# A decoder layer on one core: v projected between the turned rows, q between the chunks, and four smaller moves

## The chip, the cores and the metric

The kernel runs on one core of one Trainium2 chip. The time is the device time of one execution, in microseconds (us). A core has TensorE for matrix products (PE in the profile, its weight loads PEld), VectorE (DVE), ScalarE (ACT), GpSimd (POOL), and SyncE (SP), which issues most of the transfers. All data are float32.

## The reference, cut to what matters

One layer over x of 1024 tokens by 1024 columns (T = D = 1024), and a memory of 256 tokens:

```
n = rmsnorm(x, g_mix);  x_ssm, u, v, q = split(n @ w_in)       # 512 columns each
y_a = glu(gelu(s5_ssm(x_ssm)) @ w_glu + b_glu)                 # diagonal state-space scan
y_b = gelu(u) * spatial(rmsnorm(gelu(v), g_sgu))               # mixing within chunks of 128 tokens
y_c = attention(q, rmsnorm(mem, g_mem) @ w_kv)                 # 4 heads of 128
h   = x + (sum_i sigmoid(n @ w_gate + b_gate)_i * (y_i @ w_branch_i)) @ w_out
xf  = rmsnorm(h, g_ffn)
groups, experts = xf @ w_group + b_group, xf @ w_router + b_router    # top group of 8, top 2 of its 8 experts
out = rmsnorm(h + weighted sum of 2 experts(xf), g_final)             # 64 experts, 1024 -> 512 -> 1024
```

## The kernel before, in words

The program is one block with a hand-written instruction order for each engine; semaphores join them. Tokens go in NT = 8 tiles of 128. PSUM has four banks that ScalarE empties (`act_bank`) and four that VectorE empties (`dve_bank`). Every bank filling is a numbered job: `act_jobs` and `dve_jobs` list them in order (`plan`), job n uses bank n mod 4, and TensorE waits before job n until job n - 3 is drained. So the order of the list is the order on TensorE, on the draining engine, and in the waits.

**Head.** SP loads the eight tiles of x, small parameters and `w_ssm`. ScalarE takes squares and a root of four tiles at a time, VectorE normalizes them, TensorE turns each tile into two banks, and ScalarE and VectorE copy one bank each into `nT`. After all eight, TensorE turns the raw lambda (job "lam"); VectorE then computes the discretized parameters, with one visit to ScalarE for the sine; GpSimd raises the phases and fills `Lmat`. TensorE meanwhile projects x_ssm (job "ssm_proj", 8 blocks), then makes the convolution kernel (job "kernel", line 793), then tile 0 of v, then "bin" (it waits for `states_in_made` of GpSimd, line 630). SP copies the kernel into `toep`, after which the four chunks run: `chunk_in` (turn, then the state product of line 824) and `chunk_out` (line 833 with `toep`, line 842 with the state). VectorE runs `rotate`, `add_out` and `make_state` for each chunk in turn. Tiles 1 to 4 of v stand between chunks 1 and 0's output, tile 5 after the last chunk, tiles 6 and 7 after the turning of y ("ysT"), and all eight blocks of q after those. Then come the GLU, the memory's norm and turning, k and vm.

**Attention.** TensorE makes k (4 blocks) and both blocks of vm, waits until they are drained, and then makes the scores of tile 0; the softmax of tile 0 (VectorE, ScalarE, VectorE) follows, and only then the transposes of its probabilities. Later tiles have the scores of the next tile and a block of u between them.

**Gates, branches, output.** After a loop of eight gate steps, TensorE waits for `merged`, both halves of w_out and the router's weights, and then projects: `project(i)` is tile i of merged @ w_out (32 matrix instructions). For each tile: `project(i + 1)`, `rank(i - 1)` (the count of earlier tokens of the same expert, by a triangular matrix), the turning of the normed tile, its logits. VectorE: norm of tile i, `residual(i + 1)`, `place(i - 1)` (the token's row in the expert table), then `choose(i)` once the logits are there. The running sum `chosen` of the chosen experts enters the rank.

**Experts.** A unit is up to 32 tokens of one expert. Weights stream into four slots; SP refills a slot when TensorE has read it (`gu_ready`, `y_ready`).

The order that the change touches stands in this table of jobs:

```
(act_jobs, (("x", NT), ("ssm_proj", STEP), ("v0", 1), ("bin", 8), ("in0", 2), ("in1", 2), ("v1", 4),
            ("in2", 2), ("in3", 2), ("v5", 1), ("ysT", STEP // 2), ("v6", 2), ("q", 2 * KW),
            ("glu_b", 6), ("mem", NM), ("glu_b6", 2), ("k", HEADS), ("vm", NM),
            ("scores", 2 * NT + 2 * KW), ("gates", 6 * KD), ("xfT", 2 * NT))),
```

Of the kernel before, what the change touches and what calls it, by code (L numbers as in the profile page):

```python
# [27 lines left out]
ALU = mybir.AluOpType  # L28
# [75 lines left out]
def program(nc, x, mem, g_mix, g_mem, w_in, w_gate, b_gate, lam_re, lam_im, log_dt, b_re, b_im,  # L104
# [3 lines left out]
    with ctx:  # L108
# [52 lines left out]
        x_rows = mid_store[:, :].rearrange("p (i d) -> p i d", i=NT)  # L161
# [39 lines left out]
        w_ssm, w_glu_s = tiles(7, KD), tiles(4, KW)  # L201
# [42 lines left out]
        block_at, row_at = now[:, 342:344], now[:, 344:346]  # L244
# [80 lines left out]
        for family, rows in (  # L325
            (act_jobs, (("x", NT), ("ssm_proj", STEP), ("v0", 1), ("bin", 8), ("in0", 2), ("in1", 2), ("v1", 4),
                        ("in2", 2), ("in3", 2), ("v5", 1), ("ysT", STEP // 2), ("v6", 2), ("q", 2 * KW),
                        ("glu_b", 6), ("mem", NM), ("glu_b6", 2), ("k", HEADS), ("vm", NM),
                        ("scores", 2 * NT + 2 * KW), ("gates", 6 * KD), ("xfT", 2 * NT))),
# [13 lines left out]

        def v_job(i):
            return job(act_jobs, "v0") if i == 0 else job(act_jobs, f"v{1 if i < 5 else 5 if i < 6 else 6}",
                                                          i - (1 if i < 5 else 5 if i < 6 else 6))
# [4 lines left out]
        def score_job(i):  # L351

            return job(act_jobs, "scores", 3 * i - 1 if i else 0)

        def u_job(i):
            return job(act_jobs, "scores", 3 * i + 4 if i < NT - 1 else 3 * i + 2)
# [15 lines left out]
        def logits_job(i):  # L372

            return job(dve_jobs, "out", 4 * i + 4 if i < NT - 1 else 4 * i + 2)

        def rank_job(i):

            return job(dve_jobs, "out", 4 * i + 7 if i < NT - 2 else 29 + 2 * (i - NT + 2))
# [23 lines left out]
        def _(sp):  # L402
            x_tiles = x[0].rearrange("(i p) d -> i p d", p=P)
            for i in range(NT):
                sp.dma_start(x_rows[:, i], x_tiles[i]).then_inc(x_row_loaded[i], 16)

            def columns(w, a, n):
                return w[:, a:a + n].rearrange("(k p) n -> p k n", p=P)

# [7 lines left out]
            sp.dma_start(w_ssm, columns(w_in[0], 0, W)).then_inc(w_loaded["ssm"], 16)  # L417
# [4 lines left out]
            for n, v in enumerate((c_re, c_im)):  # L422
                for z in range(2):
                    for g2 in range(2):
                        sp.dma_start(c_raw[:, 2 * n + z, 64 * g2:64 * g2 + 64],
                                      v[0].rearrange("(g z j) h p -> z g (j h) p", z=2, g=2)[z, g2]
                                      ).then_inc(ssm_loaded, 16)
            sp.dma_start(lane_row[:, :], bc(d_skip[0], 0, P)).then_inc(bias_loaded, 16)
# [9 lines left out]
            sp.wait_ge(act_filled, jobs_end(act_jobs, "ssm_proj"))  # L438
            sp.dma_start(w_v, columns(w_in[0], 2 * W, W)).then_inc(w_loaded["v"], 16)
# [17 lines left out]
            sp.wait_ge(act_filled, jobs_end(act_jobs, "q"))  # L457
# [18 lines left out]
            sp.wait_ge(act_filled, jobs_end(act_jobs, "vm"))  # L476
# [102 lines left out]
        def _(pool):  # L579
# [71 lines left out]
            pool.wait_ge(act_filled, jobs_end(act_jobs, "vm"))  # L651
# [85 lines left out]
        def _(pe):  # L737
# [25 lines left out]
            for i in range(NT):  # L763
                pe.wait_ge(row_normed[i % 2], i // 2 + 1)
                bank = act_bank_for(job(act_jobs, "x", i))
                turn(bank, [x_rows[:, i, k * P:(k + 1) * P] for k in range(4)]).then_inc(act_filled, 1)
                bank = dve_bank_for(job(dve_jobs, "x", i))
                turn(bank, [x_rows[:, i, k * P:(k + 1) * P] for k in range(4, 8)]).then_inc(dve_filled, 1)

            pe.wait_ge(act_drained, NT)  # L770
            pe.wait_ge(dve_drained, NT)
# [4 lines left out]
            for s in range(STEP):  # L776
                if s == 2:
                    pe.wait_ge(ssm_loaded, 16 * N_SSM)
                    bank = dve_bank_for(job(dve_jobs, "c"))
                    turn(bank, [c_raw[:, n] for n in range(4)]).then_inc(dve_filled, 1)  # L780
                bank = act_bank_for(job(act_jobs, "ssm_proj", s))
                ins = accumulate(bank[:, :], [(nT_phase[:, k, s], w_ssm[:, k]) for k in range(KD)])
                ins.then_inc(act_filled, 1)
# [3 lines left out]
            for q in range(QUADS):  # L787
                for g2 in range(2):
# [6 lines left out]
                    ins.then_inc(dve_filled, 1)  # L795

            pe.wait_ge(w_loaded["v"], 16)

            def v_tiles(a, b):
                for i in range(a, b):  # L800
                    bank = act_bank_for(v_job(i))
                    ins = accumulate(bank[:, :], [(nT[:, k, i * P:(i + 1) * P], w_v[:, k]) for k in range(KD)])
                    ins.then_inc(act_filled, 1)

            v_tiles(0, 1)
# [40 lines left out]

            chunk_in(0)
            chunk_in(1)
            v_tiles(1, 5)
# [4 lines left out]
            chunk_in(3)  # L854
            chunk_out(2)
            chunk_out(3)
            v_tiles(5, 6)
# [7 lines left out]
            v_tiles(6, NT)  # L865

# [901 lines left out]
```

## Time and profile before

| | |
|---|---|
| median of 3 runs | 2270.11 us (2269.36 to 2274.81) |
| profiled execution, its own time | 2267.0 us |
| its span | 2265.1 us |
| granted TensorE clock, mean | 0.908 of full speed |
| busy: TensorE matrix, VectorE, ScalarE, GpSimd | 1794.9, 475.1, 254.8, 258.2 us |
| head and mixers, up to the last gate step | 0 to 965.5 us |
| output projection and routing | 965.5 to about 1146 us |
| experts | about 1146 to 2199 us |
| last norm and store | 2199 to 2265 us |

Times in the rows are counted from the start of the span. A duration in a row is that of the whole group of instructions ("x32" is 32 of them); a float32 product of one pair of operands stands as two matrix instructions. The bracket at the end of a row is the engine's idle time before it and what ended it. TensorE runs at one of two levels, 1.2 and 2.4 GHz, which the column PEclk shows as 0.50 and 1.00.

### The profile page before, as it was taken

The numbers are of one execution on the slowest core, as the hardware profiler recorded it, in microseconds if no ns is written. First come the engines' busy times: TensorE is split into PE (matmuls) and PEld (weight loads), VectorE is DVE, ScalarE is ACT, GpSimd is POOL, SyncE is SP. The second block draws the span as 40 slices with busy tenths as digits, with TensorE's granted clock in tenths as the row PEclk, the third lists the DMA queues.
The fourth block names the chain that finished last, engine by engine and source line by source line (L and its number), as shares of the span: only waits on it lengthen the run. The fifth ranks groups of instructions, "written<-read, shape, count | busy, mean of one in ns | idle before, by whom it ended". The sixth has DMA issues, their size and how long they took to land.

```text
span 2265.1 us, 38820 instructions
## 1 busy us (share of the span) xinstructions
PE 1794.9 (79%) x13852; PEld 1000.1 (44%) x13853; DVE 475.1 (21%) x1140; ACT 254.8 (11%) x538; POOL 258.2 (11%) x377
## 2 busy tenths in 40 slices
PE   6998999999999999989757777777777776455550
PEld 4655445654444444435434444444444453232220
DVE  6554012431011111025521001010011010000006
ACT  3112212410000000001100000000000000000003
POOL 2940000000000000001111111111111110000014
PEclk9998999999999999999879889899999899676775
DMA  6412013011111110055479999989999979999985
GB/s 224 122 40 107 4 36 105 23 44 42 42 42 42 42 42 29 8 189 197 184 275 400 409 409 406 401 308 374 405 397 369 391 283 419 415 416 420 422 334 210
DMA packets 152743, 510.96 MB, mean 226 GB/s; under 512 B 34352, under 2 KB 84016, under 8 KB 135792
## 3 DMA queue, kind: packets, MB, share of 16 engines
q1 hardware_dynamic: 122096, 461.36, 52.5%
q0 software_dynamic: 8768, 27.02, 3.4%
q10 hardware_dynamic: 21840, 22.06, 2.8%
q8 instruction: 23, 0.38, 0.1%
q14 instruction: 16, 0.13, 0.0%
HBM read 479.71 MB, written 34.35 MB: 227 GB/s over the span
## 4 chain that ended last, share of the span: by engine, by line
PE 56%; DMA 18%; SPq 11%; issue 5%; DVE 5%; ACTq 2%; ACT 1%; POOL 1%; POOLq 0%; DVEq 0%
PE act_bank L751 27%; PE dve_bank L751 14%; DMA gain_b<-xf_rows,gather_idx 11%; SPq L553 5%; PE act_bank L1045 4%; DMA unit_results<-spatialT 3%; SPq L499 3%; PE dve_bank L758 3%; PE act_bank L1059 2%; SPq L503 2%; DMA tokens<-expert_token_table 2%; PE dve_bank L1059 2%; ACTq L1247 1%; DMA unit_results<-lane_row 1%; DVE unit L1311 1%
## 5 line engine op out<-in xcount | busy, mean ns | idle before, releaser
L751 PE MATMUL act_bank<-norm_store,unit 128*128 128x512 f32 x1024 | 448.9, 592 | 0.0
L751 PEld LDWEIGHTS act_bank<-norm_store,unit 128*128 128x128 f32 x1024 | 194.6, 190 | 241.1 <-issue 240.6
L1045 PE MATMUL act_bank<-unit,gain_a 128*32 128x256 f32 x3520 | 207.3, 388 | 26.2 <-issue 26.1
L758 PE MATMUL dve_bank<-ident,gain_b 32*128 32x32 f32 x808 | 73.8, 235 | 179.8 <-DMA gain_b<-xf_rows,gather_idx 179.6
L1059 PE MATMUL act_bank<-unit,gain_a 128*32 128x256 f32 x2208 | 175.4, 471 | 39.6 <-DVE gain_a L1717 39.6
L1715 DVE TENSOR_TENSOR gain_a<-gain_a,act_bank 128x128 f32<-128x128 f32 x100 | 28.8, 288 | 757.0 <-ACT gain_a L1240 739.0
L1045 PEld LDWEIGHTS act_bank<-unit,gain_a 128*32 128x32 f32 x3520 | 123.6, 113 | 111.4 <-issue 53.5
L758 PEld LDWEIGHTS dve_bank<-ident,gain_b 32*128 32x128 f32 x808 | 64.1, 151 | 223.8 <-issue 223.8
L1059 PEld LDWEIGHTS act_bank<-unit,gain_a 128*32 128x32 f32 x2208 | 90.2, 130 | 97.4 <-issue 81.4
L1593 DVE TENSOR_TENSOR rows_store<-dve_bank,rows_store 128x512 f32<-128x512 f32 x48 | 33.2, 692 | 431.1 <-PE dve_bank L751 431.1
L751 PE MATMUL dve_bank<-unit,mid_store 128*128 128x512 f32 x256 | 113.4, 602 | 9.0 <-DMA unit<-in_w_router 9.0
L751 PE MATMUL dve_bank<-unit,unit 128*128 128x512 f32 x256 | 115.1, 592 | 0.0
L688 POOL COPY gather_idx<-tokens 32x1 int32 x100 | 17.8, 178 | 841.7 <-PE dve_bank L758 580.8
L751 PE MATMUL act_bank<-unit,norm_store 128*128 128x512 f32 x256 | 113.5, 603 | 0.0
L751 PE MATMUL dve_bank<-unit 128*128 128x512 f32 (+1 forms) x320 | 104.0, 474 | 6.2 <-ACT unit L1092 6.2
L692 POOL DMA_INDIRECT gain_b<-xf_rows,gather_idx x101 | 94.7, 938 | 83.4 <-POOL gather_idx L688 83.4
L1045 PE MATMUL act_bank<-norm_store,gain_a 128*32 128x256 f32 x1344 | 83.3, 403 | 21.6 <-issue 21.6
L1045 PE MATMUL act_bank<-mid_store,gain_a 128*32 128x256 f32 x1536 | 91.5, 391 | 10.1 <-issue 10.1
L1059 PE MATMUL dve_bank<-rows_store,gain_a 128*32 128x256 f32 x992 | 75.2, 454 | 17.8 <-DVE gain_a L1717 17.8
L751 PEld LDWEIGHTS act_bank<-unit,norm_store 128*128 128x128 f32 x256 | 64.7, 255 | 44.9 <-issue 30.5
L1205 ACT ACTIVATE rows_store<-act_bank,gate_bias_now 128x512 f32<-128x512 f32 x48 | 33.0, 687 | 417.6 <-PE act_bank L751 417.5
L751 PEld LDWEIGHTS dve_bank<-unit,mid_store 128*128 128x128 f32 x256 | 48.9, 193 | 68.9 <-issue 68.9
(227 smaller groups left out, 1474.5 us busy)
## 6 DMA issues: line engine op xcount, KB each, us to landing
unit<-in_w SPq DMA_DIRECT2D x112, 2048.0 KB
norm_store<-in_w SPq DMA_DIRECT2D x32, 2048.0 KB
mid_store<-in_w SPq DMA_DIRECT2D x32, 2048.0 KB
rows_store<-in_w SPq DMA_DIRECT2D x16, 2048.0 KB
unit<-in_w_gate SPq DMA_DIRECT2D x24, 512.0 KB, 5.2
unit<-in_w_in SPq DMA_DIRECT2D x4, 2048.0 KB, 8.9
unit_results<-unit POOLq DMA_DIRECT2D x4, 2048.0 KB, 13.4
unit_results<-spatialT ACTq DMA_DIRECT2D x220, 32.0 KB
```

The costliest lines, as they stand in the source:

```text
L499: sp.dma_start(w13[s][:, z].rearrange("p k n -> p (k n)"), w_up[z].rearrange("e (p k) n -> p (e k n)", p=P)).then_inc(up_loaded[s], 16)
L503: sp.dma_start(w2s[s], w_down.rearrange("e (k p) n -> p (e k) n", p=P)).then_inc(down_loaded[s], 16)
L553: sp.dma_start(tokens[:, s], table_of[bass.ds(e, 1)].rearrange("e p n -> (e p) n")).then_inc(tokens_loaded[s], 16)
L692: pool.indirect_dma_start(xg, None, xf_dram, bass.IndirectOffsetOnAxis(ap=gather_idx[:, 0:1], axis=0), bounds_check=T - 1, oob_is_err=Fals ...
L751: ins = nc.tensor.matmul(out_, stationary, moving, start=first and n == 0, stop=n == len(pairs) - 1)
L758: ins = nc.tensor.transpose(bank[:, n * rows:(n + 1) * rows], block_, ident[0:rows, 0:rows])
L1045: ins = nc.tensor.matmul(act_bank[0][h * CAP:(h + 1) * CAP, 0:2 * FQ].rearrange("t (w n) -> t w n", w=2), xT[:, k], w13[s][:, :, k, h * FQ ...
L1059: ins = nc.tensor.matmul(y_bank[s][z * CAP:(z + 1) * CAP, 0:DQ], hidT[:, j], w2s[s][:, j, z * DQ:(z + 1) * DQ], start=j == 0, stop=j == QU ...
L1205: drained(nc.scalar.activation(gates[n % 4], act_bank[g % 4][:, :], ACT.Sigmoid, bias=gate_bias_now[:, s, i:i + 1]))
L1247: act.dma_start(y_dram[bass.ds(u * CAP, CAP), z * DQ:(z + 1) * DQ], y_rows[s][z * CAP:(z + 1) * CAP]).then_inc(per_slot["y_stored"][s], 16)
L1593: v.tensor_tensor(parts[i], dve_bank[b % 4][:, :], gates[n % 4], ALU.mult).then_inc(dve_drained, 1)
L1715: v.tensor_tensor(hid, silu_g, act_bank[0][:, FQ:2 * FQ], ALU.mult).then_inc(per_slot["hid_ready"][s], 1)
```

## The change

1. `w_v` is loaded after the fourth tile of x; `w_ssm` goes to another buffer (unit 5) and is loaded last of the early parameters. Tile i of x lies at another place of `mid_store`, so that v's rows don't overwrite rows that are still to be turned.
2. TensorE: turn x 0, 1; v 0; turn x 2, 3; v 1; turn x 4 to 7; lam; v 2 to 4; the turning of C; v 5 to 7; ssm_proj 0 to 2; kernel; ssm_proj 3 to 7; bin. ScalarE and VectorE follow this order: ScalarE takes the squares of tiles 4 to 7 after it has copied x 0 and 1, and the sine after v 2; VectorE copies x 0 and x 1 between norms, and x 2 to 7 after the last norm.
3. q: blocks 0 and 1 stand where v 1 to 4 stood; block 2 ahead of the output of chunk 2, block 3 ahead of that of chunk 3, block 4 after it, blocks 5 to 7 after ysT. The memory's squares follow block 5.
4. vm block 1 comes after the scores of tile 0; the wait for it stands ahead of its first use.
5. The wait for the router's weights moves from ahead of the projections to ahead of the first logits. `rank(i - 1)` moves behind the turning of tile i.
6. The norm of tile 7 comes ahead of the choice of tile 6; tile 6's rank and place come after the choice of tile 7, and tile 7's rank adds tile 6's choice by further products with `ones` in place of `chosen`. `row_at` gets two buffers.

The core of the diff:

```diff
-            (act_jobs, (("x", NT), ("ssm_proj", STEP), ("v0", 1), ("bin", 8), ("in0", 2), ("in1", 2), ("v1", 4),
-                        ("in2", 2), ("in3", 2), ("v5", 1), ("ysT", STEP // 2), ("v6", 2), ("q", 2 * KW),
+            (act_jobs, (("x0", 2), ("v0", 1), ("x2", 2), ("v1", 1), ("x4", 4), ("v2", 6), ("ssm_proj", STEP),
+                        ("bin", 8), ("in0", 2), ("in1", 2), ("q0", 2), ("in2", 2), ("in3", 2), ("q2", 1), ("q3", 1),
+                        ("q4", 1), ("ysT", STEP // 2), ("q5", 3),
...
             for i in range(NT):
-                sp.dma_start(x_rows[:, i], x_tiles[i]).then_inc(x_row_loaded[i], 16)
+                if i == 4:
+                    sp.dma_start(w_v, columns(w_in[0], 2 * W, W)).then_inc(w_loaded["v"], 16)
+                sp.dma_start(x_rows[i], x_tiles[i]).then_inc(x_row_loaded[i], 16)
...
+            x_turn(0, 2)
+            pe.wait_ge(w_loaded["v"], 16)
+            v_tiles(0, 1)
+            x_turn(2, 4)
+            v_tiles(1, 2)
+            x_turn(4, NT)
             pe.wait_ge(lam_loaded, 16 * 4)
             bank = dve_bank_for(job(dve_jobs, "lam"))
             turn(bank, [lam_raw[:, n] for n in range(2)], PAIRS).then_inc(dve_filled, 1)
+            v_tiles(2, 5)
...
             chunk_in(0)
             chunk_in(1)
-            v_tiles(1, 5)
+            pe.wait_ge(w_loaded["q"], 16)
+            q_part(0, 2)
             pe.wait_ge(toep_made, 16 * STEP)
             chunk_out(0)
             chunk_in(2)
             chunk_out(1)
             chunk_in(3)
+            q_part(2, 3)
             chunk_out(2)
+            q_part(3, 4)
             chunk_out(3)
-            v_tiles(5, 6)
+            q_part(4, 5)
...
+            vm_part(0)
+            pe.wait_ge(act_drained, jobs_end(act_jobs, "k"))
             scores(0)
+            vm_part(1)
...
             pe.wait_ge(w_loaded["out_hi"], 16)
-            pe.wait_ge(w_loaded["route"], 32)
...
+                if i == NT - 1:
+                    for c in range(2):
+                        nc.tensor.matmul(bank[:, 0:E], ones, hot[:, i - 1, c], start=False, stop=False)
...
-                if i:
-                    rank(i - 1)
                 pe.wait_ge(xf_made, i + 1)
...
+                if i and i < NT - 1:
+                    rank(i - 1)
+                if i == 0:
+                    pe.wait_ge(w_loaded["route"], 32)
...
             for i in range(NT):
+                if i < NT - 1:
+                    row_norm(i)
                     residual(i + 1)
+                    if i:
+                        place(i - 1)
+                if i == NT - 2:
+                    row_norm(NT - 1)
```

## Rows read from the trace of the kernel before

**Rows 1.** Stretches: length; busy PE, PEld, DVE, ACT, POOL; PEclk, DMA share, GB/s.
```profile
32.39:106.41 74.02, 74.02 (x278) 52.94 (x276) 50.91 (x127) 7.79 (x12) 56.09 (x81) 1.00 0.42 149
151.96:199.64 47.68, 35.11 (x273) 32.54 (x272) 35.56 (x54) 6.93 (x12) 6.34 (x5) 0.79 0.08 28
365.16:377.74 12.58, 7.28 (x26) 6.04 (x26) 5.03 (x8) 3.81 (x10) 0.78 (x1) 0.73 0.55 147
400.00:960.00 560.00, 560.00 (x1472) 263.72 (x1471) 94.89 (x143) 63.50 (x107) 1.51 (x8) 1.00 0.13 36
965.50:1004.04 38.54, 29.58 (x65) 12.99 (x65) 7.20 (x14) 2.73 (x4) 1.54 (x4) 0.87 0.64 239
1111.74:1139.36 27.62, 13.71 (x73) 12.31 (x71) 17.30 (x73) 5.16 (x9) 3.88 (x4) 0.62 0.97 383
1163.00:2199.00 1036.00, 721.75 (x10448) 428.80 (x10440) 91.10 (x300) 66.18 (x200) 110.39 (x198) 0.88 0.98 389
```

**Rows 2.** Timeline of PE in the head: start, duration, group, idle before.
```profile
16.58 1.09 PE L758 MATMUL act_bank<-ident,mid_store 128*128 128x128 f32 x4 [16.58 <-DVE mid_store L1287]
...
116.23 3.68 PE L824 MATMUL dve_bank<-unit,unit 128*64 128x128 f32 x32 [3.63 <-ACT unit L1092]
...
122.50 1.97 PE L824 MATMUL dve_bank<-unit,unit 128*64 128x128 f32 x32 [0.69 <-ACT unit L1092]
...
151.96 1.95 PE L833 MATMUL dve_bank<-unit,unit 128*128 128x128 f32 x16
...
193.21 6.50 PE L842 MATMUL dve_bank<-unit,gain_b 64*128 64x128 f32 x32 [8.12 <-DVE gain_b L1481]
```

**Rows 3.** Timelines of DVE and POOL in the head, columns as in rows 2.
```profile
32.50 0.19 DVE L1335 COPY unit<-dve_bank 128x32 f32<-128x32 f32 x1 [0.40 <-PE dve_bank L758]
...
81.97 0.06 DVE L1435 MEMSET table_mark<- 128x1 f32 x1
...
129.90 0.20 DVE L1451 MEMSET gain_b<- 128x4 f32 x2 [29.77 <-POOLq L633]
...
157.38 0.69 DVE L1488 TENSOR_TENSOR mid_store<-mid_store,dve_bank 128x512 f32<-128x512 f32 x1 [0.66 <-PE dve_bank L842]
...
192.46 0.69 DVE L1481 TENSOR_TENSOR gain_b<-unit 128x508 f32<-128x508 f32 x1
...
107.19 0.72 POOL L600 TENSOR_TENSOR unit<-gain_b 128x256 f32<-128x256 f32 x1
```

**Rows 4.** The chain that ended last, head: start, duration, what.
```profile
88.28 11.15 PE dve_bank L793 x128
```

**Rows 5.** Timeline of SP's queue, then transfers to 420 us: KB each, us to landing.
```profile
113.02 0.63 SPq L447 DMA_DIRECT2D unit<-in_w_in  x1
...
unit<-in_w_in SPq DMA_DIRECT2D x4, 2048.0 KB, 8.9
```

**Rows 6.** Timeline of PE at the first scores.
```profile
372.46 1.94 PE L758 MATMUL dve_bank<-ident,rows_store 128*128 128x128 f32 x8 [4.61 <-issue]
```

**Rows 7.** Timelines of SP and PE where the projections begin.
```profile
967.95 0.82 SPq L511 DMA_DIRECT2D rows_store<-in_x  x2
...
974.50 29.70 PE L751 MATMUL dve_bank<-unit,mid_store 128*128 128x512 f32 x64 [8.96 <-DMA unit<-in_w_router]
```

**Rows 8.** Timeline of PE, one turn of the routing loop.
```profile
1021.44 0.55 PE L1000 MATMUL dve_bank<-unit 128*128 128x64 f32 x4
...
1022.05 1.04 PE L758 MATMUL act_bank<-ident,rows_store 128*128 128x128 f32 x8
1023.84 2.00 PE L751 MATMUL dve_bank<-unit 128*128 128x72 f32 x16 [0.74 <-ACT unit L1092]
```

**Rows 9.** Timeline of PE and the chain at the last tile.
```profile
1126.93 3.69 PE L751 MATMUL dve_bank<-unit 128*128 128x72 f32 x16 [0.75 <-ACT unit L1092]
...
1134.69 1.11 PE L1000 MATMUL dve_bank<-unit 128*128 128x64 f32 x4 [4.07 <-DVE unit L1649]
...
1139.19 0.18 DVE table_row L1631
```

More of the change, by code:

```diff
@@ L243, in program @@
         top, mark = now[:, 338:340], now[:, 340:342]
-        block_at, row_at = now[:, 342:344], now[:, 344:346]
+        block_at, row_base = now[:, 342:344], [now[:, 344 + 2 * n:346 + 2 * n] for n in range(2)]
         spatial_raw = mid_store[:, 0:512].rearrange("t (h s) -> t h s", h=HEADS)
@@ L774, in _ @@
             turn(bank, [lam_raw[:, n] for n in range(2)], PAIRS).then_inc(dve_filled, 1)
-            pe.wait_ge(w_loaded["ssm"], 16)
[L776 to L783, printed above, removed]
+            v_tiles(2, 5)
+            pe.wait_ge(ssm_loaded, 16 * N_SSM)
+            bank = dve_bank_for(job(dve_jobs, "c"))
+            turn(bank, [c_raw[:, n] for n in range(4)]).then_inc(dve_filled, 1)
+            v_tiles(5, NT)
+            pe.wait_ge(w_loaded["ssm"], 16)
+            ssm_proj(0, 3)
             pe.wait_ge(tables_made, 1)
@@ L795, in _ @@
                     ins.then_inc(dve_filled, 1)
[L797 to L805, printed above, removed]
+            ssm_proj(3, STEP)
             pe.wait_ge(states_in_made, 1)
@@ L845, in chunk_out, with q_part @@
                     ins.then_inc(dve_filled, 1)
+            def q_part(a, b):
+                for n in range(a, b):
+                    h, z = n // 2, n % 2
+                    bank = act_bank_for(q_job(n))
+                    ins = accumulate(bank[:, :], [(w_q[:, k, h * P:(h + 1) * P], nT[:, k, z * HALF:(z + 1) * HALF])
+                                                  for k in range(KD)])
+                    ins.then_inc(act_filled, 1)
             chunk_in(0)
             chunk_in(1)
-            v_tiles(1, 5)
+            pe.wait_ge(w_loaded["q"], 16)
+            q_part(0, 2)
             pe.wait_ge(toep_made, 16 * STEP)
@@ L1022, in _ @@
                 ins.then_inc(dve_filled, 1)
+            rank(NT - 2)
             rank(NT - 1)
@@ L1171, in _ @@
                 drain("k", h, kT[:, h], width=MEM)
-            for i in range(NM):
-                drain("vm", i, vm[:, i])
+            drain("vm0", 0, vm[:, 0])
             def exponents(i):
@@ L1654, in choose, with row_norm @@
                 tt(exp_in[:, 64 + i:65 + i], top[:, 1:2], top[:, 0:1], ALU.subtract)
[L1655 removed]
+                ts(row_base[i % 2], mark, -float(T), ALU.mult, float(T * FIRST), ALU.add)
             step(v.memset(chosen, 0.0))
             dve.wait_ge(masks_made, 4)
[L1659 to L1660 removed]
+            def row_norm(i):
                 s = i % 2
@@ L1665, in _ @@
                      s, gain_a[:, :].rearrange("p (q k) -> p k q", k=KD)).then_inc(xf_made, 1)
-                if i + 1 < NT:
+            residual(0)
+            for i in range(NT):
+                if i < NT - 1:
+                    row_norm(i)
                     residual(i + 1)
-                if i:
-                    place(i - 1)
+                    if i:
+                        place(i - 1)
+                if i == NT - 2:
+                    row_norm(NT - 1)
                 n = logits_job(i)
```

195 lines of the change are left out of this document (113 added, 82 removed).

## The prediction

> **What bounds the kernel now.** I read the slices of the page first (three regimes), then busy time by stretch [rows 1], then the timelines of each engine at the places where TensorE is not busy. Up to 965.5 us the bound is TensorE: in 400 to 960 us it is busy 560.00 of 560.00 us at full clock, and nothing that the change does can shorten that. What can go are holes and half-clock time around them. In the stretch of the first projections (74.02 us) there is no hole, but ahead of it TensorE starts at 16.58 with transposes at half rate (1.09 us for four) and reaches the first projection only at 32.39 [rows 1, 2]. The chunks (151.96 to 199.64) have 12.6 us of holes at a mean clock of 0.79; the first scores 5.3 us of 12.58 at 0.73; the routing 9.0 us ahead of its first projection; the last tile 13.9 us of 27.62 at 0.62 [rows 1]. From 1163 to 2199 the DMA share is 0.98 [rows 1]: the weight stream sets the experts' pace. It restarts from TensorE's reading of the slots, so an earlier start moves it as a whole.
>
> **1 and 2, v between the turned rows.** The products stay the same; their order fills the holes. One block of v, ssm_proj or q costs 6.9 us: the stretch of 74.02 us holds nine of them, the turning of C (0.4) and the kernel, 11.15 [rows 1, 4]. Turning one tile of x costs 0.9 (eight transposes 1.04, overlapped) once the clock is up [rows 8]. New clock: turn x 0, 1 at 16.6 to 19.7 (as before), v 0 to 26.6, x 2, 3 to 28.3, v 1 to 35.2, x 4 to 7 to 38.7, lam 39.0. `w_v` stands fifth, behind the same 2 MB plus its own 2, so it lands when the eighth tile of x did, which I estimate at 16 us; that is before v 0. The squares of tiles 4 to 7 come later on ScalarE (about 19.8 to 25), and the norms end near 31, ahead of the 35.2 at which x 4 is wanted. What is late next is lam: VectorE copies it at 39.6 where it did at 32.50 [rows 3]. So VectorE's parameters and GpSimd's chain come 7.1 us later: `tables_made` 89 instead of 82, `states_in_made` 115 instead of 107.9, phases 137 instead of 129.9 [rows 3]. The extra visit to ScalarE for the sine (after v 2, drained at 46.5) lies under VectorE's own work.
>
> TensorE then runs without a wait: v 2 to 4 to 59.7, C 60.1, v 5 to 7 to 80.8, ssm_proj 0 to 2 to 101.5, kernel (wants 89) to 112.6, ssm_proj 3 to 7 to 147.1, bin (wants 115) 3.5 to 150.6. `toep` is filled by then: SP's copies began 1 us after the kernel and were done 15 us later. The wait of 3.63 us for it at 116.23, and the half clock behind it (3.68 for what took 1.97 at 122.50) go away [rows 2].
>
> **3, q in the holes.** Both `chunk_in` end near 158.5. SP issues `w_q` only when bin is filled (its buffer holds `Lmat`): 150.6 + 0.6 + 8.9 = 160.1 [rows 5], a new wait of 1.6 us, with q 0, 1 and the output of chunk 0 queued behind it. q 0, 1 end at 173.9, and a chunk's output costs 1.95 + 3.25 (half of 6.50, which ran at half clock) = 5.2 [rows 2]: 179.1. VectorE's rotate, state, rotate took 129.90 to 152.1 = 22.2; from its first input at 154.1 that ends at 176.3. So TensorE sets Y = 179.1, where before the same point was 157.3 [rows 3]. From there: in2, out1, in3 take 18.0 as before (157.3 to 175.3, VectorE's pace and 5 us of half clock in it); then q 2 to Y + 24.9, out2 to 30.1, q 3 to 37.0, out3 to 42.2, q 4 to 49.1, ysT (3.5) to 52.6, q 5 to 7 to 73.3. VectorE's last state comes at Y + 35.9 (192.46 + 0.7 against 157.3) [rows 3], under q 3. The GLU begins at 252.4 where it did at 280.8: **28.4 us less**. Bounds: 22, if one more q block runs at half clock; 34, if `w_q` is in time, the half clock in the chunks goes and the start of v is as I have it.
>
> A rule stands against this term. The Trainium skill, "TensorE: Matmul & The Clock Gate", section "Part 1: The HAM clock gate", says that the throttled state is the default and that activity releases it; the trace agrees (half rate at 16.58, and again at 116.23 behind a hole of 3.63 us). By it the small, broken products of the chunks could hold the low level into q 2 and q 3, and the gain would be some 14 us smaller. That is rival A below, worked out from the rows.
>
> **4, vm after the first scores.** The stretch from vm's end to u holds 5.30 us of idle time, and eight transposes (1.94) and eight score products at half clock [rows 1, 6]. With vm 1 (6.9 us) between, the softmax (4.61 us after the scores) is covered. Idle 5.3 and half of the 1.94 and of the 3.62 us of scores, 2.8: **8.1 us less**. Without the cover (ScalarE's exponentials later than vm 1) 2 us would be left to pay: 6 to 8.5.
>
> **5, the router's weights.** The inputs of the projections are ready when SP is released, at 967.95; they begin at 974.50 behind the route weights [rows 7]: 6.5. The 64 products took 29.70; at 6.9 us for 16 they take 27.5, so 2.2 more if the clock has not fallen. It fell during the hole (0.87 over the stretch [rows 1]); 2.5 us of hole are left, between the 0.69 after which the rate stayed high and 3.63 after which it was half [rows 2]; I take half: **7.6 us less** (6.5 to 8.7). The residual's x lands far ahead of its use.
>
> `rank` costs 0.6 (1021.44 to 1022.05), and 0.74 us of idle time wait for ScalarE between turning and logits [rows 8]. Behind the turning, rank lies in that hole, six times: **3.7 us less**. `place` comes 1.5 us later on VectorE, which has 5 us of idle time a tile. Bounds: 0 and 4.4.
>
> **6, the last tile.** With t the end of the last projection (1111.74): before, place 7 ends at t + 27.6 (1139.19 + 0.18) [rows 9]. After: turning, rank 5, logits 6 end at t + 3.4; place 5 at t + 4.0, norm 7 (3.3) at t + 7.3, choice 6 (4.6) at t + 11.9; TensorE: turning 7 at half clock to t + 9.3, copy 0.7, logits 7 (3.7 at half clock [rows 9]) to t + 13.7; tile 7's second choice 4.0 later, t + 17.7; place 6 (1.9) behind it, under the rank; rank 7: 2.83 before, with eight more matrix instructions of 0.21 at half clock 4.5, t + 22.3; place 7 (1.8) t + 24.1. **3.5 us less**. Bounds: 1 (the scatter of tile 6 goes out only 4 us before that of tile 7, and transfers are at 0.97) and 6 (full clock).
>
> **Sum.** 28.4 + 8.1 + 7.6 + 3.7 + 3.5 = 51.3 us, against the profiled execution's 2267.0: 2215.7. The median of the runs is 3.1 above that execution, so I give 2218 for it (2270.1 less 51.3 is 2218.8). With all low bounds the gain is 35.5, with all high ones 61.6.
>
> **Rivals.** A: the low clock lasts. If q 2 and q 3 run at 1.2 GHz, each costs 6.9 more; gain 37.5, time 2232.5. For it: clock 0.79 over the chunks, and half rate after holes of only 0.7 us. Against it: 6.9 us of dense products lie in each, and the rate at 16.58 was up 3 us later. B: the gain ahead of the experts is given back, since the stream of weights runs at 0.98 of the DMA for 1036 us and would be paced from a point that does not move: time 2268 to 2270, no change. Against it: the refills wait for `gu_ready`, which moves. C, the other side: the dense head runs at half clock. From 19.7 to 147.1 TensorE has sixteen blocks; at 1.2 GHz each costs 6.9 more. It decides from 7.4 blocks on (51.3 / 6.9); all sixteen would cost 110, time 2329. Against it: 560 us at 1.00 with no hole [rows 1]. D: the change is worth more, since holes between transposes and copies that I have left stay below what they were: 2204 to 2209.
>
> **How the numbers follow.** Forecast 0.78 (2209 to 2226), A 0.12, D 0.06, B 0.02, C 0.02. A difference under 0.3% (7 us) is about what a measurement of this kernel can't tell from none. Forecast, A and D are all faster by more: 0.96; B 0.02; C 0.02. The range goes from D's upper end to A: 2207 to 2232.
>
> **What would show it.** Right: first v block at about 20; kernel at 101; no hole over 2 us between 20 and 160; GLU at 252; scores of tile 0 followed by a block into `act_bank` with no hole; projections 2 us after the last merge; first expert unit some 51 us earlier, and the length from there to the end unchanged within 2 us. Wrong: PEclk under 0.8 over the chunks with a q block of 13 us; VectorE waiting for phases past 154; `w_q` landing after 165; x 4 to 7 still unnormed at 35.

## The result and the profile after

The changed kernel takes 2219.14 us (median of 4 runs, 2215.21 to 2220.36); the kernel before takes 2269.74 (4 runs on the same chip, 2268.81 to 2274.81). The ratio is 0.9774, with a 95% interval of 0.9761 to 0.9786: 50.6 us less, where 51.3 were summed up and 2218 was forecast. The profiled execution took 2220.36 us, its span 2218.3 (before 2267.0 and 2265.1), so the two traces stand 46.8 us apart. Of all runs told below one, of tok_first, took 2556.55 us at a granted clock of 0.724, where its others had 0.91 to 0.92; its median and its ratio leave it out.

Timeline of PE in the head of the changed kernel; columns as in [rows 2].

```profile
16.55 1.09 PE L764 MATMUL act_bank<-ident,mid_store 128*128 128x128 f32 x4 [16.55 <-DVE mid_store L1331]
...
19.99 8.25 PE L757 MATMUL act_bank<-unit,norm_store 128*128 128x512 f32 x16
...
148.63 3.66 PE L764 MATMUL act_bank<-ident,unit 128*128 128x128 f32 x32
...
154.38 1.97 PE L839 MATMUL dve_bank<-unit,unit 128*64 128x128 f32 x32 [1.22 <-ACT unit L1119]
...
160.66 14.00 PE L757 MATMUL act_bank<-norm_store,unit 128*128 128x512 f32 x32 [0.58 <-DMA unit<-in_w_in]
...
176.37 3.50 PE L857 MATMUL dve_bank<-unit,gain_b 64*128 64x128 f32 x32
...
193.98 7.13 PE L757 MATMUL act_bank<-norm_store,unit 128*128 128x512 f32 x16
...
229.63 20.77 PE L757 MATMUL act_bank<-norm_store,unit 128*128 128x512 f32 x48
250.23 1.02 PE L757 MATMUL act_bank<-unit 128*128 128x512 f32 x2
```

The first block of v starts at 19.99, and there is no wait until the first state product (1.22 us, line 839). The hole of 3.63 us and the half clock behind it [rows 2] are gone. The first block takes 8.25 us and the next ones 7.0: the four transposes ahead of it took 1.06 us, as at 16.55, and those behind it 0.60, so its first products still ran at the slower rate. The wait for `w_q` is 0.58 us. The last row is the first product of the GLU: 250.23, where before it was at 280.8.

Timelines of DVE in the changed kernel, columns as in [rows 3]: lam, the parameters' last step, the end of the wait for the phases.

```profile
40.99 0.18 DVE L1391 COPY unit<-dve_bank 128x32 f32<-128x32 f32 x1
...
90.37 0.06 DVE L1491 MEMSET table_mark<- 128x1 f32 x1
...
138.28 0.19 DVE L1507 MEMSET gain_b<- 128x4 f32 x2 [23.43 <-POOLq L639]
```

Each comes 8.4 to 8.5 us later than its row in [rows 3]. TensorE makes the kernel from 102.94 on and bin from 148.63, so neither waits for them.

Stretches of the changed kernel, columns as in [rows 1]: head, chunks, first scores, first projections, last tile, first expert product to near the end of the experts.

```profile
20.00:160.00 140.00, 138.04 (x551) 88.66 (x550) 66.22 (x153) 27.95 (x48) 82.80 (x104) 1.00 0.37 107
150.60:222.00 71.40, 65.57 (x439) 46.02 (x438) 55.72 (x88) 16.52 (x34) 11.80 (x10) 1.00 0.16 55
329.00:339.50 10.50, 10.50 (x37) 6.04 (x36) 5.03 (x9) 3.22 (x10) 0.78 (x1) 1.00 0.17 50
926.60:958.40 31.80, 29.36 (x66) 12.86 (x66) 7.20 (x14) 2.73 (x4) 1.53 (x4) 0.95 0.79 290
1063.00:1087.31 24.31, 15.11 (x81) 14.05 (x79) 16.85 (x71) 5.16 (x9) 3.87 (x4) 0.65 0.97 387
1108.32:2152.00 1043.68, 740.75 (x10500) 436.58 (x10500) 90.90 (x300) 66.03 (x200) 110.30 (x199) 0.86 0.97 387
```

The chunks run at 1.00 with 5.8 us without a product, where 47.68 us had 12.6 us of holes at a clock of 0.79 [rows 1]. The first scores have no hole left. The last tile looks as before: 0.65 against 0.62, and full transfers.

Timelines of the changed kernel where the projections begin, at the last tile and behind it: PE, DVE, ACT's queue, SP's queue, POOL.

```profile
929.08 29.43 PE L757 MATMUL dve_bank<-unit,mid_store 128*128 128x512 f32 x64 [2.44 <-DVE mid_store L1653]
...
1063.00 1.04 PE L764 MATMUL act_bank<-ident,rows_store 128*128 128x128 f32 x8
...
1070.38 1.97 PE L764 MATMUL act_bank<-ident,rows_store 128*128 128x128 f32 x8 [3.54 <-DVE rows_store L1331]
1073.10 3.69 PE L757 MATMUL dve_bank<-unit 128*128 128x72 f32 x16 [0.75 <-ACT unit L1119]
...
1087.14 0.17 DVE L1688 CAST table_row<-spatialT 128x2 int32<-128x2 f32 x1
...
1088.85 0.97 POOL L685 DMA_INDIRECT expert_token_table<-token_id,table_row  x1 [0.30 <-issue]
1093.50 0.33 SPq L505 DMA_DIRECT2D unit<-in_w  x1
1093.99 1.85 ACTq L1273 DMA_DIRECT2D tokens<-expert_token_table  x4
1101.20 0.18 POOL L694 COPY gather_idx<-tokens 32x1 int32 x1 [11.38 <-DMA tokens<-expert_token_table]
...
1108.32 5.10 PE L1072 MATMUL act_bank<-norm_store,gain_a 128*32 128x256 f32 x64 [1.95 <-issue]
```

The table's last row comes at 1087.14, 52.05 us earlier than in [rows 9]. From there to the first expert product it takes 21.2 us, where the kernel before took 18.0 (1139.19 to 1157.19): 3.2 us are given back. The lists of tokens (line 1273, 16 KB in four transfers) are issued 0.49 us behind 2 MB of expert 3's weights (SP, line 505) and are in use only at 1101.20. In the kernel before the tokens went out at 1144.33, ahead of those weights at 1145.55, and were in use at 1146.41. From the first expert product to the end of the span it is 1110.0 us (before 1107.9).

By parts, each as the shrinkage of its stretch between the two traces: head 30.5; GLU to the first block of u 8.3 (96.83 to 88.56); u to the end of the first 64 projection products 6.9 (6.6 of waiting, 0.3 of products); six turns of the routing loop 3.7 (108.35 to 104.65); the turning of tile 6 to the table's last row 2.7 (26.98 to 24.32). Together 52.1, less 3.2 before the experts and 2.1 in them: 46.8.

### The profile page after: what moved, and what is told of

It is laid out like the page before. It is cut to its first block, busy times and chain, and to the rows that moved or that the text cites. A ratio compares the mean times of both kernels' runs of the same rounds, so it can differ in the third digit from the quotient of the medians.

```text
span 2218.3 us, 38841 instructions
## 1 busy us (share of the span) xinstructions
PE 1793.4 (81%) x13860; PEld 994.4 (45%) x13861; DVE 473.7 (21%) x1138; ACT 255.6 (12%) x539; POOL 256.9 (12%) x377
## 4 chain that ended last, share of the span: by engine, by line
PE 57%; DMA 18%; SPq 11%; issue 5%; DVE 4%; ACTq 3%; ACT 1%; POOL 1%; POOLq 0%; DVEq 0%
PE act_bank L757 27%; PE dve_bank L757 14%; DMA gain_b<-xf_rows,gather_idx 10%; SPq L559 5%; PE act_bank L1072 5%; DMA unit_results<-spatialT 3%; SPq L505 3%; PE act_bank L1086 3%; PE dve_bank L764 3%; DMA tokens<-expert_token_table 2%; PE dve_bank L1086 2%; SPq L509 2%; ACTq L1291 2%; DMA unit_results<-lane_row 1%; PE act_bank L764 1%
## 5 line engine op out<-in xcount | busy, mean ns | idle before, releaser
L1072 PE MATMUL act_bank<-unit,gain_a 128*32 128x256 f32 x3520 | 211.4, 393 | 22.1 <-issue 21.8
L1086 PE MATMUL act_bank<-unit,gain_a 128*32 128x256 f32 x2208 | 183.0, 487 | 39.7 <-DVE gain_a L1780 38.5
```

Source lines behind the costliest of these rows:

```text
L1072: ins = nc.tensor.matmul(act_bank[0][h * CAP:(h + 1) * CAP, 0:2 * FQ].rearrange("t (w n) -> t w n", w=2), xT[:, k], w13[s][:, :, k, h * FQ ...
L1086: ins = nc.tensor.matmul(y_bank[s][z * CAP:(z + 1) * CAP, 0:DQ], hidT[:, j], w2s[s][:, j, z * DQ:(z + 1) * DQ], start=j == 0, stop=j == QU ...
```

## The experiments

The length of the experts' stage differs by up to 11 us between these executions, and doesn't follow the edits. So I read each run at three marks of its trace, and take the time of the kernel as the last test. Ratios are to the kernel before, measured on the same chip beside each; the medians come from different chips and compare only through them. The diffs show the core of each edit; the lists of jobs and the order of the draining engines follow it.

| kernel | median us | ratio (95%) | GLU starts | GLU to last table row | row to first expert product | from there to the end |
|---|---|---|---|---|---|---|
| before | 2269.74 | 1 | 280.77 | 858.4 | 18.0 | 1107.9 |
| changed | 2219.14 | 0.9774 (0.9761 to 0.9786) | 250.23 | 836.9 | 21.2 | 1110.0 |
| head_only | 2242.22 | 0.9875 (0.9846 to 0.9905) | 253.33 | 857.3 | 18.1 | 1112.2 |
| no_vm | 2227.35 | 0.9821 (0.9797 to 0.9845) | 249.02 | 844.8 | 21.2 | 1106.8 |
| no_route | 2227.46 | 0.9818 (0.9793 to 0.9843) | 249.65 | 844.2 | 21.2 | 1111.8 |
| no_rank | 2220.70 | 0.9789 (0.9764 to 0.9813) | 249.39 | 839.2 | 21.4 | 1109.6 |
| no_last | 2212.75 | 0.9770 (0.9742 to 0.9798) | 249.63 | 838.0 | 18.0 | 1105.0 |
| q_late | 2236.43 | 0.9863 (0.9835 to 0.9890) | 267.29 | 835.2 | 21.0 | 1111.6 |
| v_late | 2225.68 | 0.9819 (0.9794 to 0.9844) | 256.46 | 835.2 | 21.1 | 1112.8 |
| tok_first | 2214.09 | 0.9766 (0.9734 to 0.9798) | 249.51 | 836.9 | 15.9 | 1111.9 |
| tok_first_all | 2218.23 | 0.9780 (0.9746 to 0.9814) | 251.86 | 836.9 | 13.2 | 1115.7 |
| warm_project | 2218.68 | 0.9777 (0.9744 to 0.9810) | 248.49 | 835.0 | 21.0 | 1113.0 |
| warm_last | 2217.09 | 0.9779 (0.9740 to 0.9818) | 249.54 | 833.4 | 21.2 | 1106.4 |
| best | 2216.81 | 0.9763 (0.9745 to 0.9781) | 252.71 | 831.3 | 19.8 | 1114.8 |

### The head alone, and each later part undone

**head_only** keeps parts 1 to 3 and undoes the rest.

> Parts 1 to 3 alone (v, q, their loads); parts 4, 5 and 6 are undone. If the terms add up as stages that follow each other (theory), the GLU begins at 250.2 as in the changed kernel, the gain is 30.5 us and the time 2239 us. If the experts' stream gives back what is won ahead of it (rival), the first expert unit comes 30 us earlier and the end does not: 2255 us or more.

The head is worth 27.4 us here, about half of all; it ends 3.1 us later than in the changed kernel, though its code is the same. Timeline of PE in head_only, in the chunks:

```profile
186.13 4.46 PE L857 MATMUL dve_bank<-unit,gain_b 64*128 64x128 f32 x32 [1.10 <-DVE gain_b L1533]
...
193.17 3.68 PE L839 MATMUL dve_bank<-unit,unit 128*64 128x128 f32 x32 [0.69 <-ACT unit L1115]
196.78 8.07 PE L757 MATMUL act_bank<-norm_store,unit 128*128 128x512 f32 x16
```

In the changed kernel these groups took 3.50, 1.97 and 7.13. The clock fell between the chunks' small products, behind holes of about 1 us, and was back within one block of q. Of the twelve kernels here that have the chunks in this order, nine profiled executions ran them at 1.00 and start the GLU at 248.5 to 250.2 (v_late at 256.5), and three at 0.93 (head_only, tok_first_all, best) and start it at 251.9 to 253.3. None of their edits touches the chunks. The head is worth 27 to 32 us by that (280.77 less 253.33 and less 248.49).

**no_vm** makes both vm blocks ahead of the scores again:

```diff
             vm_part(0)
-            pe.wait_ge(act_drained, jobs_end(act_jobs, "k"))
-            scores(0)
             vm_part(1)
+            pe.wait_ge(act_drained, jobs_end(act_jobs, "vm1"))
+            scores(0)
```

> The changed kernel with both vm blocks ahead of the first scores again. Theory: the wait for the softmax of tile 0 (4.6 us), the wait for vm's drain (0.7) and half clock behind it (2.8) come back: 8.3 us slower than the changed kernel, 2227.4 us. Rival (the softmax was mostly covered otherwise): under 3 us.

Timeline of PE in no_vm at the first scores:

```profile
340.70 1.94 PE L764 MATMUL dve_bank<-ident,rows_store 128*128 128x128 f32 x8 [4.61 <-issue]
342.44 3.26 PE L935 MATMUL act_bank<-mid_store,unit 128*128 128x256 f32 x8
```

The hole of 4.61 us is back, digit for digit as in [rows 6], and the last table row comes 7.9 us later: the term of 8.1 holds.

**no_route** waits for the router's weights ahead of the projections again.

```diff
             pe.wait_ge(w_loaded["out_hi"], 16)
+            pe.wait_ge(w_loaded["route"], 32)
...
-                if i == 0:
-                    pe.wait_ge(w_loaded["route"], 32)
```

> The changed kernel with the wait for the router's weights ahead of the projections again. Theory: projections begin 6.5 us later, and the clock loss is about the same in both (the 64 products took 29.43 us with the short hole, 29.70 with the long one): 6.8 us slower, 2225.9 us. Rival: since the residual and norm of tile 0 have slack, under 3 us.

The projections wait 8.88 us where the changed kernel waits 2.44, and their 64 products take 30.27 us where they took 29.43; the row comes 7.3 us later. The term of 7.6 holds.

**no_rank** puts `rank(i - 1)` back ahead of the turning, for the first six.

```diff
+                if i and i < NT - 1:
+                    rank(i - 1)
                 pe.wait_ge(xf_made, i + 1)
...
-                if i and i < NT - 1:
-                    rank(i - 1)
```

> The changed kernel with rank(i - 1) ahead of the turning for tiles 1 to 6 again. Theory: 0.6 us a tile, six tiles: 3.7 us slower, 2222.8 us, and the period of the routing loop 18.07 us instead of 17.46. Rival (VectorE's place sets the pace): none.

The six turns take 108.37 us instead of 104.65, 3.7 as expected. But 1.4 us are won back behind them: without rank 5 between turning 6 and its logits the tail takes 22.9 us, not 24.3. Place 5 and the norm of tile 7 come earlier, so the turning of tile 7 begins 6.5 us behind that of tile 6 and not 7.4, and it takes 1.41 us and not 1.97. The part is worth 2.3 us net, and by the ratios nothing that can be told from zero.

**no_last** undoes part 6: the norm of tile 7 after the choice of tile 6, one rank and one place ahead, no further products with `ones`.

```diff
-                if i < NT - 1:
-                    row_norm(i)
+                row_norm(i)
+                if i < NT - 1:
                     residual(i + 1)
-                    if i:
-                        place(i - 1)
-                if i == NT - 2:
-                    row_norm(NT - 1)
+                if i:
+                    place(i - 1)
```

> The changed kernel with part 6 undone (norm of tile 7 after the choice of tile 6, rank and place of tile 6 ahead of the logits of tile 7). In the changed trace the last place ends 2.7 us earlier counted from the last turning of tile 6, but the scatter takes 5.1 us instead of 3.4 and the first token lists 6.8 instead of 1.6. Theory: SP now issues 2 MB of weights (rows_picked) just ahead of ScalarE's token loads and they queue behind it, which gives the 2.7 back: the time without part 6 is the same as with it, within 2 us of 2219, with token lists landing in under 2.5 us. Rival (the slow landing is chance): 2.7 us slower, 2221.8 us, and token lists as slow.

The row comes 1.1 us later, but the first expert product is earlier by 2.0 us from the GLU's start (856.0 against 858.1). Timelines of no_last: ACT's queue, SP's queue, POOL.

```profile
1093.01 1.77 ACTq L1270 DMA_DIRECT2D tokens<-expert_token_table  x4
1094.00 0.33 SPq L505 DMA_DIRECT2D unit<-in_w  x1
1094.99 0.18 POOL L694 COPY gather_idx<-tokens 32x1 int32 x1 [4.66 <-DMA tokens<-expert_token_table]
```

The tokens leave 1 us ahead of the weights and are in use 2.0 us after they were issued, not 7.2. The other traces agree. In the eight kernels here that issue those weights first (the changed kernel, no_vm, no_route, no_rank, q_late, v_late, warm_project, warm_last) the lists are in use 6.3 to 7.3 us after their issue; in the kernel before, head_only and no_last, where they go first, 2.0 to 2.2. Part 6 as made gains nothing that these runs can tell: it turns a race for the transfer engines the wrong way round.

### The two halves of the head

**q_late** puts blocks 2 to 4 of q behind the last chunk's output; **v_late** turns all eight tiles of x before the first block of v (the first lines of the diff; q_late is the rest).

```diff
-            x_turn(0, 2)
-            pe.wait_ge(w_loaded["v"], 16)
-            v_tiles(0, 1)
-            x_turn(2, 4)
-            v_tiles(1, 2)
-            x_turn(4, NT)
+            x_turn(0, NT)
...
-            v_tiles(2, 5)
+            v_tiles(0, 5)
...
             chunk_in(3)
-            q_part(2, 3)
             chunk_out(2)
-            q_part(3, 4)
             chunk_out(3)
-            q_part(4, 5)
+            q_part(2, 5)
```

> The changed kernel with q 2, 3 and 4 all behind the last chunk, none in the holes. Theory: the holes of the chunks come back with the low clock: the last chunk's output ends 42 us after that of chunk 0 (39.5 with q in the holes) and two more blocks follow it: 16 us slower, 2235 us. Rival (the clock does not fall, since it depends on what ran ahead of the chunks): 10 to 12 us slower, PEclk at 1.00 over the chunks.

> The changed kernel with all eight tiles of x turned ahead of the first block of v; VectorE keeps its order. Theory: TensorE idles for VectorE's norms as before the change and reaches lam at 32 instead of 40, but has two blocks of v (13.8 us) still to do: 5.5 us slower, 2224.6 us. Rival (the earlier lam shortens a later wait): no change.

q_late starts the GLU 17.1 us later, v_late 6.2. Timeline of PE in q_late at the last chunk, then in v_late at the turning of tile 4:

```profile
213.98 6.51 PE L857 MATMUL dve_bank<-unit,gain_b 64*128 64x128 f32 x32 [8.12 <-DVE gain_b L1533]
```

```profile
27.41 1.12 PE L764 MATMUL act_bank<-ident,mid_store 128*128 128x128 f32 x4 [4.12 <-DVE mid_store L1325]
```

The hole of 8.12 us ahead of the last output and its 6.5 us at half clock are back just as in [rows 2]. Some 17 of the head's 30 us are the q blocks in the chunks' holes, 6 the v blocks between the turned rows. The other 7 or so were not undone singly: there the hole of 3.63 us and its half clock lie, and v 1 to 4 that left the chunks.

### The tokens ahead of the weights

**tok_first** makes SP wait for the first gather before it issues the last 2 MB of expert 3; **tok_first_all** does so with all its 6 MB.

```diff
             sp.wait_ge(rows_picked, 1)
+            sp.wait_ge(tok_gathered, 16)
             expert_up(up, 3, halves=(1,))
```

In tok_first_all the loads that stand ahead of `rows_picked` move too:

```diff
-            expert_up(up, 3, halves=(0,))
...
-            expert_down(down, 3)
             sp.wait_ge(rows_picked, 1)
+            sp.wait_ge(tok_gathered, 16)
-            expert_up(up, 3, halves=(1,))
+            expert_up(up, 3)
+            expert_down(down, 3)
```

> The changed kernel with the last 2 MB of expert 3's weights issued only after the tokens of the first unit are gathered. Theory (the token lists queue behind these 2 MB): the lists land in about 1.6 us instead of 6.8, the gather stays at about 3 us, the first expert unit comes 5 us earlier, 2214 us. Rival (the 2 MB then lie in the stretch where the stream is the bound): the first unit comes earlier but the end by less than 1 us.

> The changed kernel with all of expert 3's weights (both halves of the up matrices and the down matrix, 6 MB) issued only once the token gather has landed; in the changed kernel 4 of the 6 MB are issued ahead of the scatter and 2 MB just ahead of the token loads. Theory (the weights' transfers hold up the scatter and the token lists): the scatter lands in about 3 us, not 4.9 to 5.1, token lists in 1.6, gather in 3 or less, and the first expert product starts some 2 us earlier after the table's last row than with only the last 2 MB held back (15.9 us there, 21.0 in the changed kernel), so about 13.5 to 14. Rival 1: the 6 MB arrive too late for expert 3 and the stage from the first expert product to the end, 1104 to 1112 us so far, becomes longer than 1113; the total is then no better than that with 2 MB held back (2215) or worse than the changed kernel (2219). Rival 2: the scatter is slow for its own sake and stays at 4.9.

With the last 2 MB held back the first expert product starts 15.9 us after the last row, and 13.2 us with all 6 MB held back: the scatter, 1.2 us from the end of its issue to the tokens' issue where it was 4.2, was held up too. Timelines of tok_first, ACT's queue and POOL:

```profile
1093.07 1.77 ACTq L1274 DMA_DIRECT2D tokens<-expert_token_table  x4
...
1095.07 0.18 POOL L695 COPY gather_idx<-tokens 32x1 int32 x1 [5.99 <-DMA tokens<-expert_token_table]
```

Timelines of tok_first_all: POOL and ACT's queue.

```profile
1090.43 0.96 POOL L685 DMA_INDIRECT expert_token_table<-token_id,table_row  x1 [0.30 <-issue]
...
1092.59 1.77 ACTq L1273 DMA_DIRECT2D tokens<-expert_token_table  x4
...
1094.75 0.18 POOL L694 COPY gather_idx<-tokens 32x1 int32 x1 [3.36 <-DMA tokens<-expert_token_table]
```

But the kernel gains nothing that can be measured: 0.9780 and 0.9766 against 0.9774, intervals that overlap. In tok_first_all the way from there to the end, 1115.7 us, is the longest of all, as rival 1 had it: 4 MB sent later would be missing in a stage whose transfers are 0.97 busy. The stage's own spread leaves that a possible cause and not a shown one.

### TensorE kept busy in the holes

**warm_project** and **warm_last** add transposes of the identity to a drained bank, where TensorE would wait.

```diff
+            pe.wait_ge(act_drained, jobs_end(act_jobs, "gates"))
+            for _ in range(20):
+                nc.tensor.transpose(act_bank[0][:, 0:P], ident[:, :], ident[:, :])
             pe.wait_ge(merged, 2 * KD)
...
+                if i == NT - 1:
+                    warm_bank = act_bank_for(job(act_jobs, "xfT", 2 * i))
+                    for _ in range(28):
+                        nc.tensor.transpose(warm_bank[:, 0:P], ident[:, :], ident[:, :])
                 pe.wait_ge(xf_made, i + 1)
...
             rank(NT - 2)
+            for _ in range(20):
+                nc.tensor.transpose(warm_bank[:, 0:P], ident[:, :], ident[:, :])
             rank(NT - 1)
```

> The changed kernel with 20 transposes of the identity (128 x 128) into a drained bank of PSUM, laid in the hole of 2.4 us ahead of the first projection; nothing else differs. Theory (the clock fell to 0.67 behind that hole and cost the 64 products 29.43 - 27.5 = 1.9 us): PE is busy until the projections start, the clock stays at 1.00 and the 64 products take about 27.5 us, so the table's last row comes 1.5 to 2 us earlier after the gated-unit stage. Rival: what the transposes win is nothing, since in three of the variants run so far the clock stayed up behind the same hole with nothing in it, and the products are then held by the evictions; or the transposes end later than the wait they fill and push the projections back by up to 1 us.

> The changed kernel with transposes of the identity laid in two holes of TensorE at the last tile: 28 ahead of its turn (hole 3.5 us) and 20 between the rank product of place 6 and that of place 7 (hole 2.8 us); nothing else differs. Theory (the clock halves behind these holes: the turn takes 1.97 us where 1.41 was seen, and the logits 3.7): turn, logits and the last rank product run at full clock, and the time from the turn of tile 6 to the table's last row falls from 24.3 by 3 to 5 us. Rival: most of that chain is VectorE and ScalarE work and the passing of results between engines, so that it falls by under 1 us; or the transposes run past the waits they fill, at half clock themselves (0.1 us each), and the row comes later.

Timeline of PE in warm_project:

```profile
924.73 2.35 PE L1005 MATMUL act_bank<-ident 128*128 128x128 f32 x20
927.33 27.73 PE L757 MATMUL dve_bank<-unit,mid_store 128*128 128x512 f32 x64 [0.25 <-DVE mid_store L1656]
```

Timeline of PE in warm_last:

```profile
1065.97 3.22 PE L1039 MATMUL act_bank<-ident 128*128 128x128 f32 x28
1069.73 1.09 PE L764 MATMUL act_bank<-ident,rows_store 128*128 128x128 f32 x8 [0.53 <-DVE rows_store L1337]
1071.62 2.00 PE L757 MATMUL dve_bank<-unit 128*128 128x72 f32 x16 [0.80 <-ACT unit L1125]
```

Both did what was expected: the 64 products take 27.73 us, not 29.43, and the last tile's turning and logits 1.09 and 2.00, not 1.97 and 3.69. The last row comes 1.9 and 3.5 us earlier from the GLU. Neither moves the kernel's ratio (0.9777 and 0.9779), whose intervals reach 7 to 9 us to each side and could not show so little.

### All of it together

> Three edits on the changed kernel at once: expert 3's last 2 MB of weights issued only once the token gather has landed, 20 transposes of the identity in the hole ahead of the first projection, and 28 and 20 of them in the two holes of the last tile. Alone they moved the table's last row after the gated-unit stage by 0, 1.9 and 3.5 us, and the first expert product after that row by 5.1, 0 and 0. Theory (they act in different places and add up): the table's last row starts about 831.5 us after the first product of the gated-unit stage (836.9 in the changed kernel), the first expert product about 16 us after that row ends (21.0), at 1097 to 1099 in all. Of these 10.5 us, the experts' stage, whose weights are read at 370 to 390 GB/s with the 16 DMA engines nearly always busy, may keep some: its length from the first expert product has been 1105 to 1116 us, so 2204 to 2214, most likely 2209, a ratio to before of 0.972 to 0.977. Rival (the stage is bound by the stream of weights, and whoever starts it early only waits inside it): the stage is 1115 us or longer and the median is 2215 to 2220, as with the single edits.

The last row comes at 831.3 us from the GLU, as the sum had it (831.5). The first expert product then takes 19.8 us and not 16. Stretches of best, then of tok_first, columns as in [rows 1]:

```profile
1089.00:1093.00 4.00, 0.00 (x0) 0.00 (x0) 1.87 (x7) 0.00 (x0) 0.00 (x0) 0.50 1.02 413
1093.00:1097.00 4.00, 0.00 (x0) 0.00 (x0) 0.00 (x0) 1.49 (x2) 0.18 (x1) 0.50 0.17 58
```

```profile
1089.00:1093.00 4.00, 0.00 (x0) 0.00 (x0) 3.72 (x10) 0.00 (x0) 0.09 (x1) 0.50 0.78 309
1093.00:1097.00 4.00, 0.00 (x0) 0.00 (x0) 0.42 (x3) 1.49 (x2) 1.01 (x2) 0.50 0.04 7
```

Timelines of POOL and ACT's queue in best:

```profile
1086.30 0.97 POOL L686 DMA_INDIRECT expert_token_table<-token_id,table_row  x1 [0.30 <-issue]
1091.78 1.98 ACTq L1283 DMA_DIRECT2D tokens<-expert_token_table  x4
1096.69 0.18 POOL L695 COPY gather_idx<-tokens 32x1 int32 x1 [9.42 <-DMA tokens<-expert_token_table]
```

The weights that SP issues once the last projection has been read fill the transfer engines to some 30 us behind it (about 1093 in best, a little earlier in tok_first). Under it the scatter is slow, and the lists of tokens come in when it is over. In best the tokens left at 1091.78 and were in use at 1096.69, 4.9 us later; in tok_first, sent at 1093.07 behind the end of the stream, 2.0 us later. Of the 5.6 us by which the last row comes earlier from the GLU than in tok_first, 1.7 are left at the first expert product (851.1 us from the GLU against 852.8). The median of best, 2216.81, cannot be told from the changed kernel's. Its stage of 1114.8 us and its median are as the rival had them, or near. But that stage is of the slowest of its five executions, whose GLU also starts 2.5 us late, with the chunks at 0.93; two others took 2210.28 and 2211.75 us, and the ratio, 0.9763, lies in the range of 0.972 to 0.977 that the theory gave. So best does not decide between the two. No version here beats the changed kernel by more than a measurement can tell.

## Why the prediction was right

**Head.** 28.4 forecast, 30.5 measured (27.4 in head_only). The first block of v cost 8.25 us instead of 6.9, since it began at the slower rate, and lam, tables and phases came 1.3 to 1.4 us behind their forecast with it. They had cover. Y, the end of chunk 0's output, was forecast at 179.1 and came at 179.8. The GLU came 2.2 us ahead of 252.4, because I had left 18.0 us "as before" for in2, out1, in3, half clock included; they took 14.1 (to 193.98) at full clock. q_late shows that the filling of the chunks' holes is the largest single piece.

**Rival A** (the low clock lasts) did not come. Where the clock did fall, in head_only, block 2 of q took 8.07 us, 0.9 more than 7.13 and not 6.9 more. The Trainium skill, "TensorE: Matmul & The Clock Gate", section "Part 1: The HAM clock gate", has the throttled level as the default that activity releases. The trace agrees: the clock rose again during that block, and out2 behind it took 1.95 and 3.50 us, as at full clock.

**vm, router's weights, rank.** 8.1, 7.6, 3.7 forecast; 8.3, 6.9, 3.7 measured, and 7.9, 7.3, 2.3 when undone one at a time. For the projections I took half of a clock loss of 2.2 us; 1.7 of it was there in the profiled execution and none in q_late, v_late and no_last with the same hole. The prediction set the length of a hole against the clock behind it, but its own rows already have both answers for 0.7 us (1.97 at 122.50 [rows 2], and the "half rate after holes of only 0.7 us" of its rival A); the length alone does not settle it. The rank's 3.7 stands in the loop, but I had not seen that the same move lays rank 5 into the tail, where it costs 1.4. The two terms also share one piece: six ranks were counted here, and the tail was counted from the end of the last projection, with rank 5 (0.65 us before) inside it.

**Last tile.** 3.5 forecast, 2.7 measured to the last row; the row was done at t + 24.3 where t + 24.1 was laid out. (The 2.7 counts from the turning of tile 6, the 3.5 from the end of the last projection; by the latter mark it is 3.3.) I had put the low bound down to the scatters of tiles 6 and 7 coming close together; what was hit was the transfer behind them, the token lists, by the weights. no_last shows that the part loses 2.0 us at the first expert product.

**Rival B** (given back in the stream) came in small: 3.2 us between row and first product, 2.1 in the experts, 5.3 of 52.1. The first expert product came 48.9 us earlier where some 51 were forecast. The refills do move with the earlier start, as was argued; over the six kernels whose first expert product came by 1106, the length from there to the end is 1111 us on average, and over the seven later ones as well. **Rival C** had no ground: 138.04 of 140.00 us busy, and only the start of the first block was slow. **Rival D**, 2204 to 2209, did not come either: the gains beyond the forecast in the head were given back ahead of the experts and in them.

The forecast is 1.1 us off, partly by luck: the head gave 2 more, the experts took 5, and the medians stand 4 us further apart than the two profiled executions. The range, 2207 to 2232, was also drawn more tightly than its terms: all low bounds together (35.5) give 2234.6, and D's upper end was 2209.

## What to carry to other kernels

Fill holes with products that are owed anyway: blocks of q and v in the waits of a serial chain gave some 23 of the 50 us (q_late 17, v_late 6), and saved the half clock behind the holes as well. When a tail of small steps ends in small transfers, look at what the big ones do at that moment: once the tail was shorter than the weight stream, 1.7 of 5.6 us were left of a further cut. Read such an edit at the mark where it acts, since a later stage that jitters by 10 us hides it.

## What the hardware showed

- The clock differed behind the same code. Behind one and the same hole of 2.44 us ahead of the projections the 64 products took 29.4 us in six kernels and 27.73 in three (no_last, q_late, v_late), as much as with the hole filled. In the chunks the same code ran at 1.00 in nine executions and at 0.93 in three. Timeline of PE in no_last at the projections, to set beside that of the changed kernel:

```profile
928.47 27.73 PE L757 MATMUL dve_bank<-unit,mid_store 128*128 128x512 f32 x64 [2.44 <-DVE mid_store L1650]
```

- In these runs a small transfer waited for the large ones. Sent 0.49 us behind 2 MB of weights on another queue, lists of 16 KB were in use after 7.2 us; sent ahead of them, after 2.0. The Trainium skill, "DMA: Bandwidth & Descriptors", section "Queues, rings and completion order", says that each transfer engine takes turns between its queues packet by packet, and drains a whole packet, typically 9 to 17 descriptors, before it switches. The trace of the changed kernel has the 2 MB as 128 records of 16 KB, on average 8 for each of 16 engines; the first record of the lists starts 4.2 us after their issue (1.0 in no_last), and 100 of their 192 between 1100.0 and 1100.5, where the weights' last record ends at 1100.99. Whether that is one packet of weights per engine or something else, no run here shows; why the lists are held for 5 us longer was not tried.
- Transposes of the identity alone kept TensorE's clock at its upper level through holes of 2.4 and 3.5 us: 20 took 2.35 us in warm_project and 28 took 3.22 in warm_last, and what stood behind them ran at full clock.
